# In which order the first sixteen weight chunks are asked for

## What is computed

```
hn = rms_norm(x, norm_pre[0])          # x: 256 x 2048
q, k, v, g = split(hn @ w_in_a[0], 4)  # w_in_a[0]: 2048 x 8192
```

## Time and profile before

| what | us |
|---|---|
| median of three runs | 2192.85 |
| the profiled execution | 2191.04 |
| its span, first to last instruction | 2189.3 |
| TensorE busy | 2170.5 (99%) |
| VectorE busy | 1381.8 (63%) |
| ScalarE busy | 1166.0 (53%) |
| granted TensorE clock, mean | 0.997 |
| HBM read | 389.96 MB, 179 GB/s over the span |

### The profile page before, as it was taken

One profiled execution on the slowest core, in us unless ns is written; L12 is line 12 of the kernel. 1 busy time (PEld: TensorE's weight loads), 2 busy tenths in 40 slices (PEclk: granted clock), 3 DMA queues, 4 the chain that ended last, 5 costly groups with the idle time before them and its releaser, 6 DMA issues.

```text
span 2189.3 us, 29405 instructions
## 1 busy us (share of the span) xinstructions
PE 2170.5 (99%) x12096; PEld 1873.3 (86%) x12096; DVE 1381.8 (63%) x1750; ACT 1166.0 (53%) x1543; POOL 15.2 (1%) x30
## 2 busy tenths in 40 slices
PE   8999999999999999999999999999999999999998
PEld 7888888888888888888888888888888888888886
DVE  5655555558787656577757787577565544565655
ACT  5555554655665555566545554555444443454443
POOL 1000000000000000000000000000000000000000
PEclk9999999999999999999999999999999999999999
DMA  6655556455556444565555555556666556666654
GB/s 215 191 177 178 175 167 181 162 187 184 188 167 175 145 144 150 179 202 192 184 182 173 165 171 175 186 161 189 188 190 192 191 193 193 187 189 191 206 185 148
DMA packets 223205, 393.98 MB, mean 180 GB/s; under 512 B 20937, under 2 KB 42962, under 8 KB 222944
## 3 DMA queue, kind: packets, MB, share of 16 engines
q1 hardware_dynamic: 221664, 388.35, 56.3%
q0 software_dynamic: 1264, 3.70, 0.5%
q10 hardware_dynamic: 144, 0.07, 0.0%
HBM read 389.96 MB, written 2.11 MB: 179 GB/s over the span
## 4 chain that ended last, share of the span: by engine, by line
PE 94%; DVE 3%; ACT 1%; issue 1%; DMA 1%; SPq 0%; DVEq 0%; ACTq 0%
PE ps L896 94%; DVE WL L1440 1%; PE ps L906 1%; DMA RAW<-in_w_in_a 0%; ACT WH L1165 0%; DVE TMP L1440 0%; DVE gT L1443 0%; ACT gT L1165 0%; DVE gT L1440 0%; DVE ACC L1440 0%; ACT SQ L1165 0%; ACT F L1178 0%; DVE RAWL L1443 0%; DVE TMPG L1443 0%; DMA GN<-gains 0%
## 5 line engine op out<-in xcount | busy, mean ns | idle before, releaser
L1440 DVE TENSOR_TENSOR WL<-RAW,WH 128x1024 fp32r<-128x1024 f32 (+1 forms) x733 | 886.4, 1220 | 448.6 <-ACT WH L1165 446.8
L896 PE MATMUL ps<-H,WH 128*128 128x512 f32 x3152 | 1113.6, 398 | 5.9 <-DVE WL L1440 4.8
L1165 ACT ACTIVATE WH<-RAW 128x1024 fp32r<-128x1024 f32 (+1 forms) x733 | 767.9, 1055 | 657.7 <-PE ps L896 642.3
L896 PE MATMUL ps<-H,WL 128*128 128x256 f32 x3152 | 879.5, 279 | 0.0
L896 PEld LDWEIGHTS ps<-H,WH 128*128 128x128 f32 x3152 | 592.0, 188 | 145.9 <-DVE WL L1440 7.3
L896 PEld LDWEIGHTS ps<-H,WL 128*128 128x128 f32 x3152 | 594.9, 189 | 1.2
L896 PE MATMUL ps<-O,WH 128*128 128x512 f32 (+1 forms) x1376 | 475.5, 392 | 0.1
L896 PE MATMUL ps<-O,WL 128*128 128x256 f32 x1344 | 375.8, 280 | 0.0
L896 PEld LDWEIGHTS ps<-O,WH 128*128 128x128 f32 x1376 | 255.9, 188 | 57.9 <-DVE WL L1440 0.7
L896 PEld LDWEIGHTS ps<-O,WL 128*128 128x128 f32 x1344 | 253.6, 189 | 0.6
L896 PE MATMUL ps<-WH,ACTS 128*128 128x512 f32 x704 | 218.3, 390 | 0.0
(11 more groups left out here) (227 smaller groups left out, 1392.3 us busy)
## 6 DMA issues: line engine op xcount, KB each, us to landing
RAW<-in_w_in_a SPq DMA_DIRECT2D x127, 512.0 KB, 3.6
RAW<-in_w_in SPq DMA_DIRECT2D x96, 512.0 KB, 3.6
RAW<-in_w_gate SPq DMA_DIRECT2D x88, 512.0 KB, 3.5
RAW<-in_w_up SPq DMA_DIRECT2D x88, 512.0 KB, 3.5
RAW<-in_w_down SPq DMA_DIRECT2D x88, 512.0 KB, 3.6
RAW<-in_w_ple_gate SPq DMA_DIRECT2D x64, 512.0 KB, 3.6
RAW<-in_w_in_b SPq DMA_DIRECT2D x40, 512.0 KB, 3.6
RAW<-in_w_out_a SPq DMA_DIRECT2D x32, 512.0 KB, 3.6
```

Source lines behind the costliest of these rows:

```text
L896: return e.matmul(o, l, r, start=start, stop=True, skip_group_check=True)
L1165: return e.activation(o, i, f, **kw)
L1440: return e.tensor_tensor(o, x, y, op)
```

## The change

Two places of `sync_engine`. The trigger at `split_lo` of i now asks for chunk i+3 for every i below 13, so for chunks 3 to 15, and a counter `asked` remembers the last one. The trigger after the second half of chunk i asks for nothing below chunk 16; from there on it asks for all chunks that are not asked for yet, up to i+7. `load_chunk` with its waits is as it was.

```
             for what, m in FIRST:
                 (load_x if what == "x" else load_chunk)(m)
+            asked = 2
             for kind, *args in steps:
                 if kind == "split_lo":
-                    if args[0] + 3 < NRAW:
+                    if args[0] + 3 < PACED:
                         load_chunk(args[0] + 3)
+                        asked = args[0] + 3
                     if args[0] in (1, 2):
                         load_x(3 + args[0])
                 elif kind == "chunk":
                     i, _, _, _, part = args
-                    if part and i + NRAW in loads:
-                        load_chunk(i + NRAW)
+                    while part and PACED <= asked + 1 <= min(i + NRAW, len(chunks) - 1):
+                        asked += 1
+                        if asked in loads:
+                            load_chunk(asked)
```

## The result

The changed kernel takes **2184.34 us** (median of six runs, 2184.12 to 2184.76) against 2193.06 for the kernel before (six runs, 2191.73 to 2194.74). The ratio is 0.996 with a 95% interval of 0.9948 to 0.9972, so 8.7 us less, somewhere between 6.1 and 11.4. The forecast was 2185.3, with 2184.3 to 2186.3 as its own range, which the measurement meets at its lower edge, and 2183.8 to 2187.8 for 8 cases in 10; forecast gain 7.5, which lies inside the interval. The changed kernel was profiled at 2184.15 us, with a span of 2182.4.

What follows compares the result with a forecast made beforehand. Two requests looking one chunk ahead were taken to cost TensorE 7.52 us between 22 and 33 us. The sum 0 + 0 - 7.5 gave 2185.3 us for the median, range 2184.3 to 2186.3 (8 in 10: 2183.8 to 2187.8).

Steps and rivals of the forecast that it cites:

- Where the time lay: TensorE from 22 to 33 us: one hole with 4.28 us of idle and some slow matmuls, costing 7.52 us.
- the 7.52: TensorE, chunk 4's to chunk 6's transposes: 14.04 us instead of 6.52; parts 3.06 idle, 4.20, and 0.26 slower first matmuls.
- Two transfers in series: Chunk 5 hangs on chunk 4's low part, chunk 6 on chunk 5's, each through a whole transfer (4.64 and 4.63 us).
- The low clock isn't a cost of its own here.: TensorE before chunk 6: its low part comes at 32.71 by a chain without matmuls, so the whole 7.52 hangs on requests.
- the offset of 1.81 us: The profiled execution lay 1.81 us below the median of 2192.85, so its forecast 2183.5 became 2185.3 for the median.
- The landings: DMA transfers land in order of request, 1.3 us apart: chunk 5 at 17.3, x5 at 18.6, chunk 6 at 19.9.
- What is late next: The high and low splits of chunks 5 to 8, just in time: taken as 0, bounds 0 and about 2 us.
- x4: TensorE's transposes at 16.97: x4 lands at 15.97, a cover of 1.0 us, not delayed by the new requests: 0.
- The wait of 0.8: TensorE at x4, by the skill page's latency: x4 lands 1.8 us later, TensorE waits 0.8, gain only 6.7.
- Nothing given back: The 7.5 us gain lasts to the end; rival, 0.6 to 3 us lost at x4 or splits: 2186 to 2188.3, chance 0.15.

Runs made afterwards that it cites:

- the second profile: The kernel before, unchanged, profiled and timed once more: 2192.92 us, ratio 1.0001.
- The two kernels with one wait: The kernel before with only chunk 7's request moved behind chunk 5 and x5, 2189.24 us; or only chunk 8's moved behind chunk 6, 2190.48 us.
- the filled kernel: The kernel before with small matmuls of zeros in TensorE's waits ahead of chunks 5 and 6: 2191.80 us, and 2191.84 when run again.
- the first single request: The kernel before with only chunk 7's request moved behind chunk 5 and x5; chunk 6 still behind chunk 8: 2189.24 us.
- the first kernel without pacing: The changed kernel with chunks 3 to 6, x4, x5 requested behind the first requests, chunks 7 to 15 when their slot is free: 2183.85 us.
- the two chunks ahead: The changed kernel with chunks 3 to 15 requested at the low part two chunks before instead of three: 2189.98 us.
- the kernel with the late x4: The changed kernel with x4 (x tiles 8 to 11) requested behind chunk 5 instead of ahead of it: 2186.98 us.

## Why the prediction was right

- **Where the time lay.** Right. The hole from 22 to 33 us is gone and all else stayed: after the copy of `q0` the first profile before has 2189.3 - 41.84 = 2147.5 us left, the changed kernel 2182.4 - 34.60 = 2147.8. Of the 7.52, I had put 0.26 down to slower first matmuls. Only 0.11 is: from chunk 6's start to its transposes it was 1.52 us, and 1.41 without a wait. The other 0.15 lies ahead of the first wait: from chunk 4's transposes to the end of its last matmul it was 2.00 us (22.23), where the next chunk starts after 1.85 in the changed kernel. The sum isn't touched.
- **Two transfers in series.** Right. Between the starts of chunks 5 and 6 lay 7.46 and 7.48 us in two executions, at different clocks; with the clock held up, the hole was still 14.35 to 14.54.
- **"The low clock isn't a cost of its own here."** This step failed in part. It is true when the clock falls ahead of chunk 5, as in the execution I read: 6.8 us of low clock, nothing lost. When it falls ahead of chunk 6, no wait lies behind it, and the second profile lost 24.08 - 21.61 = 2.5 us by it. The medians may hold both kinds; one profile of each doesn't tell in what share. The Trainium skill ("TensorE: Matmul & The Clock Gate", section "Terms") puts the penalty of a throttled clock at the throttled time times what is missing of the ratio, so half of it here. The two kernels with one wait agree (1.7 of 3.4 us); the profiles of before don't (0 of 6.8, and 2.5 of 6.8 where the rule gives 3.4, since there 1.9 us of it passed while TensorE waited).
- **Why 8.7 and not 7.5.** This is open in part. The interval of the gain, 6.1 to 11.4, holds both. I took the hole of one execution for that of the median. With the clock held up the distance to the changed kernel was still 8.5 us, of which 7.8 and 8.0 lay in the hole, so some tenths are transfers in series that last longer than in the execution I read, and the low clock's share, 0.6 to 1.2 us by the filled kernel, isn't clear of noise. That the median came within 1 us of the forecast is luck in part: it needs the offset of 1.81 us between the profiled execution and three runs.
- **The landings.** Chunk 5, x5 and chunk 6 landed 1.1 to 1.2 us later than worked out: x4 itself landed 0.6 later, chunk 5 came 1.9 us behind it and not 1.3, and from there on the spacing of 1.3 held. The margins took it: 0.8 us were left ahead of ScalarE's turn for chunk 5, where I had 1.8, and 0.5 at x4, where I had 1.0.
- **What is late next.** Right: the splits, with 0.7 us to spare at chunks 5 to 7 and 0.27 at chunk 8 (forecast: 0.5 to 0.6, and 0.2), and no wait at any of them.
- **x4.** The two requests behind it held it up little, if at all: it took 4.9 to 7.2 us in the five profiles with chunk 5 and x5 requested behind it at about 12, and 4.8 to 6.4 in the six of kernels without. The wait of 0.8 that the latency in the Trainium skill ("DMA: Bandwidth & Descriptors", section "Latency and other measured facts") would have made did not come. But the cover was thin: 0.5 us in the first profile of the changed kernel and none in the second, where TensorE waited 0.2, and asked for 2.5 us later x4 was late.
- **Nothing given back.** Right within what the profiles can tell. The lead is 7.36 us at chunk 6's transposes and 6.9 at the end of the span; after the copy of `q0` eleven of the fourteen profiles need 2147.0 to 2148.4 us, so the difference of 0.3 there is scatter. (The other three are the first single request with 2149.6 and the first kernel without pacing with 2149.0, neither followed up, and the two chunks ahead with 2152.0.)

The runs of before spread over 7.6 us in all groups together (2189.81 to 2197.4, 89 runs), those of the changed kernel over 1.8 (2182.97 to 2184.76, eleven runs). A profile of one execution of the kernel before was one draw from that.

## What to carry to other kernels

In a queue that is served in order, a request with a far-off wait makes every request behind it as late as itself: write the requests in the order in which their waits come true, and check each for how many steps it really looks ahead. That distance must cover landing and preparation, here 3.5 to 7.4 us plus 2.3, which three chunks of 2.8 to 3.3 us did and two did not. Before pricing a stretch of low clock, ask what ends it: in these profiles it was free ahead of another wait, and with work behind it half of it counted, and one profile may show only one of the two.

## What was not expected of the hardware

- The clock fell during 3.06 us of idle, 2.2 us after its start, in one execution and stayed up through 3.13 in another of the same kernel. In the two kernels with one wait, of 3.39 and 3.71 us, it fell only when TensorE had worked again for 1.5 and 0.7 us. It stayed low for 6.8, 6.8, 3.4 and 3.4 us in the four profiles that show it.
- In the kernel with the late x4, whose longest wait in this stretch was 1.5 us in its one profile, three of eight runs had a mean clock of 0.997 or 0.998, against 0.999 in the others.
- With requests queued closely (DMA engines 0.92 busy on the mean from 12 to 20 us in the changed kernel) half a megabyte took 6.5 to 7.4 us to land (7.2 and 8.2 for x4 and x5 in its second profile), and 3.7 and 3.8 with nothing ahead of it in the queue (chunks 7 and 8 of the kernel before).
